# Feed-forward in four groups of 4, 6, 6 and 6 tiles instead of three of 6, 8 and 8, with the scaled rows kept

## The reference, cut to what matters

```python
def swiglu(x, w_gate, w_up, w_down):
    return (jax.nn.silu(x @ w_gate) * (x @ w_up)) @ w_down
...
x = x + 0.5 * rmsnorm(f1, ffn1_post_g)     # f1 = swiglu(rmsnorm(x, ffn1_pre_g), ...), inner width 2816
x = x + rmsnorm(y, mix_post_g)             # y: four mixers between two projections
x = x + 0.5 * rmsnorm(f2, ffn2_post_g)     # f2: a second swiglu
```

## Time and profile before

| | |
|---|---|
| median of 3 runs | 1140.06 us (1137.98 to 1143.65) |
| profiled execution | 1142.68 us, its span 1140.9 us, so 1.8 us lie around the span |
| PE busy | 1079.9 us (95%), 9138 matmuls |
| DVE, ACT, POOL busy | 798.3 us (70%), 461.8 us (40%), 277.4 us (24%) |
| mean granted TensorE clock | 0.957 |
| DMA | 92.04 MB, 81 GB/s on average |

### The profile page before, as it was taken

The page is one execution under the profiler, slowest core; times in us unless marked ns, Lnnn a source line. Parts: engine busy times, 40 slices in busy tenths (PEclk is TensorE's granted clock), DMA queues, the critical chain, the costliest instruction groups (busy, mean ns, idle before and its releaser), DMA issues. The chain is left out here.

```text
span 1140.9 us, 23394 instructions
## 1 busy us (share of the span) xinstructions
PE 1079.9 (95%) x9138; PEld 1056.2 (93%) x9138; DVE 798.3 (70%) x1224; ACT 461.8 (40%) x776; POOL 277.4 (24%) x217
## 2 busy tenths in 40 slices
PE   6999999999999999999699989899999999999996
PEld 6999999999999999999577789899999999999995
DVE  5667699436975787888669536767578983399646
ACT  6423456315654344522134433433235552256520
POOL 0220665034530000120213000004126531355101
PEclk9999999999999889999779989889999999999998
DMA  6222222422324121232601003103142324223212
GB/s 215 92 84 96 88 102 74 134 88 75 110 74 130 38 71 56 79 76 75 67 2 39 2 1 95 56 19 111 55 130 76 109 75 146 75 74 110 92 56 79
DMA packets 35400, 92.04 MB, mean 81 GB/s; under 512 B 10368, under 2 KB 12928, under 8 KB 35328
## 3 DMA queue, kind: packets, MB, share of 16 engines
q1 hardware_dynamic: 34320, 88.78, 25.3%
q10 hardware_dynamic: 1008, 2.27, 0.6%
HBM read 87.76 MB, written 3.28 MB: 80 GB/s over the span
## 5 line engine op out<-in xcount | busy, mean ns | idle before, releaser
L315 PE MATMUL ps<-xh,wh 128*128 128x272 f32 x816 | 194.7, 301 | 16.0 <-DVE xl L499 8.6
L811 PE MATMUL ps<-seven,wh 128*128 128x272 f32 x1024 | 195.5, 287 | 6.6 <-ACT silu L825 6.6
L315 PE MATMUL ps<-xh,wl 128*128 128x272 f32 x816 | 190.9, 297 | 0.0
L315 PE MATMUL ps<-xl,wh 128*128 128x272 f32 x816 | 190.1, 296 | 0.0
L298 DVE TENSOR_TENSOR wl<-raw,wh 128x1024 fp32r<-128x1024 f32 (+1 forms) x99 | 119.1, 1205 | 100.5 <-ACT wh L293 100.1
L811 PEld LDWEIGHTS ps<-seven,wh 128*128 128x128 f32 x1024 | 159.7, 188 | 7.4 <-ACT silu L825 7.4
L293 ACT ACTIVATE wh<-raw 128x1024 fp32r<-128x1024 f32 (+1 forms) x99 | 100.2, 1020 | 158.8 <-PE ps L315 73.5
L315 PE MATMUL ps<-hh,wh 128*128 128x272 f32 x704 | 157.9, 291 | 0.4 <-DVE hl L863 0.4
L315 PEld LDWEIGHTS ps<-xh,wh 128*128 128x128 f32 x816 | 140.7, 197 | 18.6 <-DVE wl L298 9.0
L315 PE MATMUL ps<-hh,wl 128*128 128x272 f32 x704 | 156.5, 290 | 0.0
L315 PE MATMUL ps<-hl,wh 128*128 128x272 f32 x704 | 156.4, 289 | 0.0
(11 more groups left out here) (348 smaller groups left out, 1920.6 us busy)
## 6 DMA issues: line engine op xcount, KB each, us to landing
raw<-in_w_gu SPq DMA_DIRECT2D x88, 512.0 KB, 3.7
raw<-in_w_d SPq DMA_DIRECT2D x32, 512.0 KB, 3.6
raw<-in_w_in SPq DMA_DIRECT2D x19, 512.0 KB, 3.6
raw<-in_w_d SPq DMA_DIRECT2D x16, 384.0 KB, 3.0
raw<-in_w_out SPq DMA_DIRECT2D x8, 512.0 KB, 3.6
out_y<-x SPq DMA_DIRECT2D x16, 136.0 KB, 1.8
x<-in_x ACTq DMA_DIRECT2D x4, 272.0 KB, 5.5
x<-in_x SPq DMA_DIRECT2D x4, 272.0 KB, 6.6
```

What stands on the lines that cost most here:

```text
L315: last = pe.matmul(out[:, n], left[:, s, j], right[:, j, n * H:n * H + H], start=first and opens and j == order[0], stop=final and closes ...
L811: last = pe.matmul(out, left[:, j], right[:, j], start=m in (0, 1, 3) and j == 0 and left is hi and right is high, stop=j == 3 and left is ...
```

## The change

`GROUPS` becomes 4, 6, 6, 6 tiles. Per stage 18 tiles instead of 16 are made by seven products and 4 instead of 6 by plain units, and there are four passes of down units instead of three. Since group 0 uses only rows 0 to 3 of `hh` and `hl`, the eight scaled rows are kept in rows 4 to 7 of both (`xs`); the second scaling goes away. The four pairs of sums are now made in four units, one pair in each, instead of eight. The order at the end of the groups is changed in `fast_act` and `fast_dve`.

```diff
-GROUPS = ((0, 6), (6, 8), (14, 8))
+GROUPS = ((0, 4), (4, 6), (10, 6), (16, 6))
...
+        xs = (at("ffn", "xs0", [4, N], offset=HH + 4 * 4 * N), at("ffn", "xs1", [4, N], offset=HH + 12 * 4 * N))
...
# fast_sp: first transfer of a fast group
-                        sp.wait_ge(S("q_lo"), 8 * q + 8)
+                        sp.wait_ge(S("q_lo"), 8 * q + 4)
...
# fast_act: a group's last tile
             fast_copy(act, *end, 1)
+            fast_copy(act, *end, 2)
             for d in range(4):
-                if d in (1, 2):
-                    fast_copy(act, *end, d + 1)
-                if d == 3:
-                    silu_act(act, q, nf // 2 - 1, f0, 1)
                 slots_free(act, q, g, d)
                 split_hi(act, u, 0, d, nf)
+                if d == 0:
+                    fast_copy(act, *end, 3)
+                if d == 1:
+                    silu_act(act, q, nf // 2 - 1, f0, 1)
             fast_hidden_hi(act, *end)
...
# fast_dve: a group's last tile
+            fast_first(dve, *end)
             split_lo(dve, u, 0, 0, nf)
-            fast_first(dve, *end)
+            fast_gate(dve, *end)
             split_lo(dve, u, 0, 1, nf)
-            fast_gate(dve, *end)
+            fast_hidden(dve, *end)
             split_lo(dve, u, 0, 2, nf)
-            fast_hidden(dve, *end)
+            split_lo(dve, u, 0, 3, nf)
             fast_hidden_lo(dve, *end)
-            split_lo(dve, u, 0, 3, nf)
...
# ffn_act, group 0: units, then down units
                     if s % 2:
                         silu_act(act, q, s // 4, f0, 1 + s % 4 // 2)
-                        sums_hi_act(act, q, s // 2)
+                    if s:
+                        sums_hi_act(act, q, s - 1)
...
-                    if s in (2, 4, 5, 6):
-                        rows_hi_act(act, q, (2, 4, 5, 6).index(s), u)
+                    if s == 0:
+                        sums_hi_act(act, q, 3)
+                    if s in (2, 3):
+                        rows_hi_act(act, q, 2 * s - 4, u)
+                        rows_hi_act(act, q, 2 * s - 3, u)
...
# ffn_dve, group 0: units, then down units
                     if s % 2:
                         hidden_dve(dve, q, u, s // 4, f0, 1 + s % 4 // 2)
-                        sums_lo_dve(dve, q, s // 2)
-                    else:
-                        rows_mul_dve(dve, q, s // 2, False)
+                    rows_mul_dve(dve, q, s)
+                    if s:
+                        sums_lo_dve(dve, q, s - 1)
...
                 for s in range(KD):
                     split_lo(dve, u, 0, s, nf)
                     if s == 1:
                         hidden_dve(dve, q, u - 2 * nf, 0, f0, nf - 1)
                     if s >= 2:
                         down_dve(dve, q, u, g, s - 2, n)
+                    if s == 0:
+                        sums_lo_dve(dve, q, 3)
                     if 2 <= s < 6:
                         rows_lo_dve(dve, q, s - 2)
-                    if 1 <= s < 5:
-                        rows_mul_dve(dve, q, s - 1, True)
```

More of the change, by code:

```diff
@@ L40 @@
 FT = F // P
-GROUPS = ((0, 6), (6, 8), (14, 8))
+GROUPS = ((0, 4), (4, 6), (10, 6), (16, 6))
+FAST0 = GROUPS[1][0]
+NFAST = FT - FAST0
+LAST = len(GROUPS) - 1
+SUMS = 16 + 4 * NFAST
+D_OUT = KD * LAST + 4
 G = 256
@@ L929, in fast_dve, with rows_mul_dve @@
             fast_hidden_lo(dve, q, g, nf // 2 - 1, 0)
+            fast_first(dve, *end)
             split_lo(dve, u, 0, 0, nf)
-            fast_first(dve, *end)
+            fast_gate(dve, *end)
             split_lo(dve, u, 0, 1, nf)
-            fast_gate(dve, *end)
+            fast_hidden(dve, *end)
             split_lo(dve, u, 0, 2, nf)
-            fast_hidden(dve, *end)
+            split_lo(dve, u, 0, 3, nf)
             fast_hidden_lo(dve, *end)
-            split_lo(dve, u, 0, 3, nf)
[L939 to L949, removed]
-            else:
-                dve.wait_ge(S("n_rb"), 1)
-            dve.scalar_tensor_tensor(qb[:, 0], x[:, k], par_(f"g{4 * q}", k), rb[:], MUL, MUL)
-            dve.scalar_tensor_tensor(qb[:, 1], x[:, 4 + k], par_(f"g{4 * q}", 4 + k), rb[:], MUL, MUL).then_inc(S("q_row"), 1)
+        def rows_mul_dve(dve, q, k):
+            if k == 0:
+                if q:
+                    dve.wait_ge(S("out"), 6 * 16)
+                    dve.wait_ge(S("n_rb"), mark(3, 1, 1) + 1)
+                    dve.wait_ge(S("h_x_new"), 4 * KD)
+                else:
+                    dve.wait_ge(S("n_rb"), 1)
+            dve.scalar_tensor_tensor(xs[0][:, k], x[:, k], par_(f"g{4 * q}", k), rb[:], MUL, MUL)
+            dve.scalar_tensor_tensor(xs[1][:, k], x[:, 4 + k], par_(f"g{4 * q}", 4 + k), rb[:], MUL, MUL).then_inc(S("q_row"), 1)
         def sums_hi_act(act, q, k):
-            act.wait_ge(S("f_sum"), 80 * q + 4 * k + 4)
+            act.wait_ge(S("f_sum"), SUMS * q + 4 * k + 4)
             act.activation(seven[:, 0, :, k], qq[:], ACT.Copy).then_inc(S("q_act"), 1)
@@ L963, in rows_hi_act @@
         def rows_hi_act(act, q, k, u):
[L965 removed]
+            act.wait_ge(S("q_row"), 4 * q + k + 1)
             act.wait_ge(S("unit_done"), SPL + u)
[L967 to L968 removed]
+            act.activation(xh[:, k, 0:H], xs[0][:, k, 0:H], ACT.Copy)
+            act.activation(xh[:, 4 + k], xs[1][:, k], ACT.Copy).then_inc(S("q_act"), 1)
         def rows_lo_dve(dve, q, k):
             dve.wait_ge(S("q_act"), 8 * q + 4 + k + 1)
[L972 to L973 removed]
+            dve.tensor_tensor(xl[:, k, 0:H], xs[0][:, k, 0:H], xh[:, k, 0:H].bitcast(F32), SUB)
+            dve.tensor_tensor(xl[:, 4 + k], xs[1][:, k], xh[:, 4 + k].bitcast(F32), SUB).then_inc(S("q_lo"), 1)
         def ffn_pool(pool, q, u0):
@@ L978, in ffn_pool @@
             for k in range(4):
-                pool.wait_ge(S("q_row"), 8 * q + k + 1)
+                pool.wait_ge(S("q_row"), 4 * q + k + 1)
                 if k:
                     pool.wait_ge(S("q_lo"), 8 * q + k)
-                b11, b12, b21, b22 = qb[:, 0, 0:H], qb[:, 0, H:N], qb[:, 1, 0:H], qb[:, 1, H:N]
+                b11, b12, b21, b22 = xs[0][:, k, 0:H], xs[0][:, k, H:N], xs[1][:, k, 0:H], xs[1][:, k, H:N]
                 pool.tensor_tensor(qq[:, 0], b12, b11, SUB).then_inc(done, 1)
                 pool.tensor_tensor(qq[:, 2], b22, b12, SUB).then_inc(done, 1)
-                pool.wait_ge(done, 80 * q + 4 * k + 1)
+                pool.wait_ge(done, SUMS * q + 4 * k + 1)
                 pool.tensor_tensor(qq[:, 1], b22, qq[:, 0], SUB).then_inc(done, 1)
-                pool.wait_ge(done, 80 * q + 4 * k + 3)
+                pool.wait_ge(done, SUMS * q + 4 * k + 3)
                 pool.tensor_tensor(qq[:, 3], b21, qq[:, 1], SUB).then_inc(done, 1)
             pool.wait_ge(S("unit_done"), SPL + u0 + 2 * GROUPS[0][1])
-            for g in (1, 2):
+            for g in range(1, len(GROUPS)):
                 fast_pool(pool, q, g)
@@ L1098, in down_dve @@
         def down_dve(dve, q, u, g, d, n):
-            if g == 2 and d >= 2:
+            if g == LAST and d >= 2:
                 squares_dve(dve, n, d - 1)
@@ L1129, in ffn_act @@
                         split_hi(act, u, 0, s, nf)
-                        if g == 2 and s > 4:
+                        if g == LAST and s > 4:
                             down_act(act, q, g, s - 5, n)
-                    if g == 2:
+                    if g == LAST:
                         down_act(act, q, g, 3, n)
```

56 lines of the change are left out of this document (27 added, 29 removed).

## The result

The changed kernel is slower: 1166.16 us median of 6 runs (1161.29 to 1172.38) against 1141.86 of the kernel before (1136.61 to 1145.25). The ratio is 1.0253, with a 95% interval of 1.0216 to 1.0291. The forecast was 1157 us, 1.5% above before. The medians lie 24.3 us apart, while the ratio is worth 29 us; such gaps of a few us between the two measures run through all that follows, and the text says which one it uses. The profiled execution took 1165.86 us with a span of 1164.1, 23.2 us above the span before.

A forecast was written before the change was run, and what follows sets the result against it. PE was taken as the bound, never stopping inside a fast group; -6.0 + 2.9 + 10.5 + 3.4 + 6.4 = +17.2 us gave 1157 us on the median, range 1149 to 1164, or 1143 to 1170 with rivals.

The forecast's parts named there:

- Matmuls: Fast tiles of both stages: 48 matmuls fewer at 0.125 us each, -6.0 us.
- Last tiles: Fast groups' last tiles: six waits of 1.65 us for `hl` replace 7.0 us of earlier waits, +2.9 us.
- The six waits of 1.65 us cost nothing more: Fast groups' last tiles: the clock stays full behind each wait, so no time is added.
- the clock falls at every last tile: Rival, chance 0.16: from some 2 us, each of six last-tile waits costs 1.7 us more; 1167 us, to 1170 with longer waits.
- Group 0: Group 0 of both stages: the chain of sums delays the last tile's `hl`, stalls of 3.9 and 6.6 us, +10.5 us.
- The clock behind group 0: After group 0's two stalls: PE runs at half clock for a while, 1.7 us lost each, +3.4 us.
- The ends: Ends of both stages: the smaller last group hides less DVE work, +4.1 and +2.3 us, together +6.4 us.
- The chain of sums keeps up: Rival, chance 0.12: POOL and DVE overlap better in group 0, which costs 0 to 2 us; 1144 us.
- the reordering works: Rival, chance 0.08: no stall in group 0 or at last tiles, ends half absorbed; 1130 us.

The follow-up runs named there:

- the order that takes only these waits away: The changed kernel with `hh` and `hl` of a fast group's last tile made ahead of the split of down unit 3: 1.008 of the kernel before, 1145.81 us.
- the kernel with only group 0 mended: The changed kernel with group 0's last tile ahead of the fourth pair's sums on DVE and ACT: 1.0151 of the kernel before, 1152.37 us.
- the eight filled places: The changed kernel with PE's waits for the last `hl` filled with unread matmuls, down loops unrolled: 1.0169 of the kernel before, 1153.0 us.
- the one in the old kernel alone: The kernel before, groups 6, 8, 8, with only the last tiles reordered (copy 2 ahead of split 0, `hh` ahead of split 3): 0.9927, 1129.41 us.
- the kernel with both orders mended: The changed kernel with last tiles' `hh` and `hl` ahead of split 3 and group 0's last tile ahead of the fourth sums: 0.9981, 1135.61 us.

## Where the prediction held and which step failed

**Matmuls, -6.0 us.** 9090 instead of 9138, as said. No run takes this term alone; in the changed kernel's trace six fast tiles (504 matmuls) took 63.0 us, 10.5 each, and a plain tile takes 12.

**Last tiles, +2.9 us forecast.** The mechanism was the one named: split 1 behind `fast_gate`, transfer 3 late, `hh` and `hl` behind split 3. The waits are 1.80 to 1.92 us where 1.65 were worked out, six times. That is +4.2 in place of +2.9. But this step also said "The six waits of 1.65 us cost nothing more", from one length after which the clock had stayed full. **That step failed.** In the changed kernel's trace the clock fell behind five of the six, 8.0 us in all, and the order that takes only these waits away gave 20 us for 11.2 us of waits. The rival "the clock falls at every last tile" (1167 us) was the right case; I gave it 0.16. That its number, 1167 us, lies so near is in part luck, since other terms were short too. The waits lay a fifth of a microsecond above those that I had rows for, and I took a clock that had stayed full four times as one that would do so here. Waits of the same length in the kernel with only group 0 mended had a fall behind one of six, so how many come is not settled by the length; the eight filled places show that they come from PE standing still.

**Group 0, +10.5 us forecast.** 4.52 and 6.69, together 11.2; forecast 3.9 and 6.6. The walk through the chain holds: the fourth pair's sums were forecast to start at 61.7 and started at 61.82. PE had ended its eighth unit at 64.8 and not at 66.1, and `hl` was ready at 71.7 and not at 72.2. Moving the tile ahead gave 12 us by the ratios, with its clock. What the walk missed are the late weights behind the waiting sums, 0.69 and 0.95 us in the second stage. The prediction took 4.0 us of POOL for a pair, from the earlier trace rows; the second pair there took 4.9, since two of its sums ran beside DVE's scalings and took 1.26 us each where 0.77 is usual (the scalings took 1.29 and 1.30 instead of 0.78).

**The clock behind group 0, +3.4 us forecast.** Half clock lasts 3.1 us for 14 matmuls and 4.7 for 21, where full clock needs 1.75 and 2.6: 1.4 and 2.1, together 3.5. The 1.7 us of the prediction were taken from the share of the clock; by its matmuls (19 in place of 31 in 4 us) that fall cost 1.5.

**The ends, +6.4 us forecast.** PE waits 5.31 us for DVE at the end of the first stage (forecast 5.0) and 4.26 at the very end, 2.3 more than before, and going back to 8 rows brings 7 us (2 to 12 by the intervals).

**The sum.** -6.0 + 4.2 + 11.2 + 1.6 (the late weights) + 3.5 + 8.0 (the five falls) + 7 = 29.5, against 17.2 forecast; the ratio says 29. The 7 is itself a difference of two ratios, so the agreement to half a microsecond is luck. The two profiled spans are only 23.2 apart; the one before had more half clock elsewhere: 4.0 us at 0.57 and 7 us at 0.58 are 1.00 and 0.76 at the same places of the changed kernel. The sign, the places and most sizes were right; the term for the clock was mis-sized, 3.4 us for 11.5. These 8.1 us are two thirds of the 12.3 that the sum is short.

The views of the changed kernel for these two places:

```profile
778.80:782.80 4.00, 3.93 (x31) 3.96 (x32) 3.96 (x6) 0.11 (x1) 1.31 (x1) 1.00 0.19 71
...
26.00:33.00 7.00, 7.00 (x47) 7.00 (x47) 1.34 (x4) 1.97 (x4) 0.00 (x0) 0.76 0.47 150
```

**The rivals.** "The chain of sums keeps up" and "the reordering works" are out, by the waits for L1097 and L868. With `hl` made ahead of split 3 the waits at the last tiles vanish, as the second rival's condition (`hl` ready sooner) has it.

## What to carry to other kernels

When a step is made smaller, ask what its length hid: here a shorter down unit brought forward the moment at which the last `hl` is needed, and a shorter last group laid DVE's norm bare. In an engine's hand-written order, put what the bottleneck needs next ahead of what waits for a transfer or for a third engine; two such swaps were worth 2.7% here, and the one in the old kernel alone 0.7%. When a change brings new waits of PE, work out the time with and without a fall of the clock behind each (here 1.6 us): of 23 waits between 1.67 and 2.40 us in these traces 14 were followed by one.

## What the runs showed of the hardware

The clock behind a wait of PE is not settled by the wait's length. All matmuls here are dense on both sides, 128x272.

- Six waits of 4.5 to 6.7 us for group 0's `hl`, in three kernels, were all followed by half clock, and each time the clock was at a half before PE started again (0.50 already from 71.50 to 71.70 and from 812.20 to 814.20 in the changed kernel).
- Of eleven waits of 2.33 to 2.40 us in group 0 of the second stage, over all ten traces, eight were followed by a fall; the changed kernel's was not, the one before the change was the earlier trace rows.
- Of twelve waits for L868 of 1.67 to 1.94 us, in the changed kernel and in the one with only group 0 mended, six were, five and one, though the work around them is the same.
- Of six waits of 1.48 to 1.66 us (four before the change, two for L868 in later runs) none was.

Three waits of 1.54 and 1.55 us in group 0 of the second stage were followed by a fall too, but they do not stand alone: each came 2.6 us behind another of 1.12 to 1.15 us. In the kernel with both orders mended (timeline, then the stretch):

```profile
797.79 0.51 PE L321 MATMUL ps<-hh,wh 128*128 128x272 f32 x2 [1.54 <-DVE wl L304]
```

```profile
797.70:801.70 4.00, 3.91 (x20) 3.91 (x21) 2.67 (x5) 1.97 (x5) 0.00 (x0) 0.61 0.44 135
```

There PE had stood 1.15 us until 795.23. Whether the earlier wait has a part in these falls, no run tests.

A fall comes while PE still stands or up to 1.4 us after it has started again (1.32 behind 264.71), so that a look at the first matmuls can miss it. Matmuls whose result nobody reads kept the clock at 1.00 at all eight places. What decides between 1.67 and 2.4 us stays open.
